# Two-block transformer kernel: the first three units on x without its norm, paired down units, residual updates on VectorE

## Chip, cores, metric

The kernel runs on one NeuronCore of one Trainium2 chip. The metric is the device time of one execution in microseconds.

## What is computed

Input `x` is 512 tokens by 1024 features in float32. Two pre-norm blocks follow each other, each with a feed-forward part with squared ReLU, and then a third block with three conditioned sublayers:

```python
# first block, two layers (mixer 0: dilated attention; mixer 1: latent attention)
h = rms_norm(x, norm_mix[i]); x = x + mixer(h)
h = rms_norm(x, norm_ffn[i]); x = x + sq_relu_mlp(h, w1[i], w2[i])
# second block: three sublayers (SwiGLU, attention + recurrence, SwiGLU)
h = rms_norm(x, g[2*j]) * (1 + scale) + shift
x = x + res_w * gate * rms_norm(fn(h), g[2*j + 1])
```

`rms_norm` divides each token by the root of its mean square and multiplies each feature by a gain. The mixers use 8 heads; each head of the first one has three query, three key and three value projections of 128 columns.

## The kernel before

Activations lie transposed, features on the 128 partitions, in 8 tiles `x[:, k, :]` of 512 tokens. Every weight matrix is streamed in units of 128 x 1024 (8 tiles of 128 x 128; `UNITS` of them in one order). A unit is used in split precision: ScalarE copies `raw` to `w_hi` in the rounded type fp32r (`split`, L893), the difference goes to `w_lo` (`low`: L1397 on VectorE in the attention of the first mixer, L369 on GpSimd from `U_AO + 2` on), and TensorE does three matmuls for each of the 8 steps k (L448, L449, L450: high by high, high by low, low by high). Activations are split in the same way (`h_hi`, `h_lo`). `unit` runs one unit, `unit_pair` two with their steps interleaved. Loads go out on SyncE's queue; `load_unit(u)` waits for `lo` of unit u - 3, `split(u)` for the matmuls of unit u - 3.

Each engine has one program, written out by hand, and each waits on counted semaphores (`after(name, index)`). The order within an engine is the order of the code. The parts that matter here:

- Start: `x` is squared tile by tile (`squares`, L900), summed over partitions by TensorE (L474), `inverse_root` (Ln and Exp, L921 and L923) gives the norm, `norm` makes `h_hi` and `h_lo` step by step, and then `pre_v` links (L1415 to L1431) compute a few columns of `small` from `lru_lambda` and the lambdas. The first head `a_head(0, 0, attend=False)` follows with nine units (3 queries, 3 keys, 3 values). Each query or key unit is evacuated to `a_raw` by ScalarE, squared, split, summed, normed and turned by `a_rope` (L1443 to L1456) on VectorE. Heads 1 to 7 then run as a loop in which each head projects while the one before attends. `a_head(1)` begins with unit 9.
- Feed-forward (`ffn`, two layers with four chunks each): 8 up units, `f_r` (Relu), `f_s` (square), `f_hi`, `f_lo` for each, then 8 down units that sum over the 8 tiles of `f_hi` and `f_lo`. Down unit 8 waits for `f_lo` tile by tile. VectorE also makes the conditioning (`ada_raw`, L1552) there; `condition` prepares its input.
- Sublayers: after SwiGLU or the mixer, `post_norm` scales `y` by its norm and adds it to `x`: tiles 0, 2, 3, 5, 6 on VectorE (L1799, L1801), tiles 1, 4, 7 on GpSimd (L397, L399). ScalarE squares each finished tile, TensorE sums, and `norm` makes the next input. The last `post_norm` is followed by the stores.

## Time and profile before

| | us |
|---|---|
| timed runs, median of 3 | 2627.26 (2626.61 to 2636.68) |
| profiled execution | 2632.38 |
| its span, first to last instruction | 2630.6 |
| TensorE (PE) busy | 2494.2 |
| VectorE (DVE) busy | 1270.8 |
| ScalarE (ACT) busy | 1026.6 |
| GpSimd (POOL) busy | 870.6 |

The profile is of one execution. Its lines give a start, a duration, the engine (PEld is TensorE's weight load), the line of the kernel, the operation with output and inputs, and in brackets how long the engine had been idle and what ended that. Durations of matmuls overlap by pipelining: what counts is the distance between starts. A float32 matmul (not fp32r) shows as two passes.

### The profile page before, as it was taken

The numbers are of one execution on the slowest core, as the hardware profiler recorded it, in microseconds if no ns is written. First come the engines' busy times: TensorE is split into PE (matmuls) and PEld (weight loads), VectorE is DVE, ScalarE is ACT, GpSimd is POOL, SyncE is SP. The second block draws the span as 40 slices with busy tenths as digits, with TensorE's granted clock in tenths as the row PEclk, the third lists the DMA queues.
The fourth block names the chain that finished last, engine by engine and source line by source line (L and its number), as shares of the span: only waits on it lengthen the run. The fifth ranks groups of instructions, "written<-read, shape, count | busy, mean of one in ns | idle before, by whom it ended". The sixth has DMA issues, their size and how long they took to land.

```text
span 2630.6 us, 31399 instructions
## 1 busy us (share of the span) xinstructions
PE 2494.2 (95%) x11168; PEld 1960.5 (75%) x11168; DVE 1270.8 (48%) x1737; ACT 1026.6 (39%) x1532; POOL 870.6 (33%) x369
## 2 busy tenths in 40 slices
PE   5999999999999998999999999999989968999997
PEld 3888888877888874568888878888857646688885
DVE  4766666656435555657355463201164795311114
ACT  4555555533223333544233233222344564322222
POOL 0000000024445532014455444444435334344443
PEclk8999999999999998999999999999999989999998
DMA  3222222224434521004344432223212201222221
GB/s 123 82 73 74 78 72 73 79 89 154 157 129 144 168 88 48 0 9 170 126 145 167 153 107 88 98 91 105 99 57 86 67 9 64 72 96 96 96 96 64
DMA packets 71237, 249.46 MB, mean 95 GB/s; under 512 B 9824, under 2 KB 10336, under 8 KB 70752
## 3 DMA queue, kind: packets, MB, share of 16 engines
q1 hardware_dynamic: 68912, 247.28, 28.1%
q8 instruction: 70, 1.15, 0.2%
q10 hardware_dynamic: 2224, 0.79, 0.1%
q14 instruction: 31, 0.25, 0.0%
HBM read 245.94 MB, written 2.10 MB: 94 GB/s over the span
## 4 chain that ended last, share of the span: by engine, by line
PE 86%; DVE 7%; issue 3%; ACT 2%; POOL 1%; DMA 0%; SPq 0%; ACTq 0%; DVEq 0%; POOLq 0%
PE psum L448 25%; PE psum L450 25%; PE psum L449 25%; PE psum L492 2%; PE psum L744 1%; DVE f_lo L1545 1%; PE psum L743 1%; PE psum L758 1%; PE psum L524 1%; PE psum L488 1%; PE psum L543 1%; PE psum L550 1%; DVE small L1912 1%; PE psum L817 1%; DVE y L1799 0%
## 5 line engine op out<-in xcount | busy, mean ns | idle before, releaser
L369 POOL TENSOR_TENSOR w_lo<-raw,w_hi 128x1024 fp32r<-128x1024 f32 x311 | 794.3, 2557 | 1559.1 <-ACT w_hi L893 1559.1
L448 PE MATMUL psum<-h_hi,w_hi 128*128 128x512 f32 x1856 | 740.0, 399 | 29.8 <-DVE a_k L1503 16.5
L450 PE MATMUL psum<-h_hi,w_lo 128*128 128x512 f32 x1856 | 726.4, 391 | 0.0
L449 PE MATMUL psum<-h_lo,w_hi 128*128 128x512 f32 x1856 | 725.9, 391 | 0.0
L893 ACT ACTIVATE w_hi<-raw 128x1024 fp32r<-128x1024 f32 x385 | 406.1, 1056 | 614.6 <-PE psum L450 614.3
L448 PEld LDWEIGHTS psum<-h_hi,w_hi 128*128 128x128 f32 x1856 | 351.2, 189 | 109.3 <-issue 35.4
L449 PEld LDWEIGHTS psum<-h_lo,w_hi 128*128 128x128 f32 x1856 | 351.3, 189 | 74.5 <-issue 3.4
L450 PEld LDWEIGHTS psum<-h_hi,w_lo 128*128 128x128 f32 x1856 | 350.6, 189 | 74.6
L1781 DVE TENSOR_TENSOR s_s<-s_g,psum 128x512 f32<-128x512 f32 x44 | 30.2, 687 | 399.9 <-PE psum L450 399.9
L448 PE MATMUL psum<-f_hi,w_hi 128*128 128x512 f32 x512 | 200.1, 391 | 9.4 <-DVE f_lo L1545 9.4
L450 PE MATMUL psum<-f_hi,w_lo 128*128 128x512 f32 x512 | 199.2, 389 | 0.0
L449 PE MATMUL psum<-f_lo,w_hi 128*128 128x512 f32 x512 | 199.2, 389 | 0.0
L448 PE MATMUL psum<-s_hi,w_hi 128*128 128x512 f32 x352 | 136.9, 389 | 0.0
L449 PE MATMUL psum<-s_lo,w_hi 128*128 128x512 f32 x352 | 136.9, 389 | 0.0
L450 PE MATMUL psum<-s_hi,w_lo 128*128 128x512 f32 x352 | 136.9, 389 | 0.0
L1569 DVE TENSOR_TENSOR nrm<-psum,rst 128x512 f32<-128x512 f32 x64 | 44.2, 690 | 171.7 <-PE psum L450 171.7
L1021 ACT ACTIVATE f_r<-psum 128x512 f32<-128x512 f32 x64 | 38.2, 597 | 223.4 <-PE psum L450 223.4
L962 ACT ACTIVATE a_raw<-psum 128x512 f32<-128x512 f32 x64 | 38.3, 598 | 211.9 <-PE psum L450 211.9
L448 PEld LDWEIGHTS psum<-f_hi,w_hi 128*128 128x128 f32 x512 | 96.1, 188 | 32.5 <-DVE f_lo L1545 12.8
L1552 DVE CUSTOM_DVE_ANT_0 ada_raw<-ada_raw,crow 128x1024 f32<-128x1024 f32 x72 | 117.4, 1630 | 0.0
L1542 DVE TENSOR_TENSOR f_s<-f_r,psum 128x512 f32<-128x512 f32 x64 | 43.7, 684 | 142.5 <-ACT f_r L1021 141.7
L450 PEld LDWEIGHTS psum<-f_hi,w_lo 128*128 128x128 f32 x512 | 96.1, 188 | 20.1
(286 smaller groups left out, 3399.5 us busy)
## 6 DMA issues: line engine op xcount, KB each, us to landing
raw<-stream SPq DMA_DIRECT2D x385, 512.0 KB, 3.3
ada_raw<-ada_in SPq DMA_DIRECT2D x72, 512.0 KB, 3.6
x<-x_in SPq DMA_DIRECT2D x2, 1024.0 KB, 6.4
out<-x SPq DMA_DIRECT2D x8, 256.0 KB, 2.0
a_mask<-mask_in SPq DMA_DIRECT2D x1, 1024.0 KB, 10.8
crow<-crow_in SPq DMA_DIRECT2D x2, 512.0 KB, 4.4
gatew<-gate_in ACTq DMA_DIRECT2D x2, 256.0 KB, 3.8
a_cos<-rope_in SPq DMA_DIRECT2D x1, 256.0 KB, 9.4
```

The costliest lines, as they stand in the source:

```text
L369: nc.gpsimd.tensor_tensor(w_lo[:, sl, :], raw[:, sl, :], f32(w_hi[:, sl, :]), ALU.subtract) \
L448: nc.tensor.matmul(o, whi, xh, start=start, stop=False)
L449: nc.tensor.matmul(o, whi, xl, start=False, stop=False)
L450: return nc.tensor.matmul(o, wlo, xh, start=False, stop=stop)
L492: last = nc.tensor.transpose(o[:, b * P:(b + 1) * P], src[:, b * P:(b + 1) * P], ident[:])
L893: A(w_hi[:, slot(u0), :], raw[:, slot(u0), :], ACT.Copy).then_inc(S["hi"], 1)
L962: A(a_raw[:, (par + j) % 2, :], bank((par + j) % 2), ACT.Copy).then_inc(S["A_evac"], 1)
L1021: A(f_r[:, j % 2, :], bank(j % 4), ACT.Relu).then_inc(S["F_r"], 1)
L1542: V.tensor_tensor(f_s[:, j % 2, :], f_r[:, j % 2, :], bank(j % 4), ALU.mult).then_inc(S["F_s"], 1)
L1552: V.tensor_tensor_reduce(out=ada_raw[:, j % 3, :], in0=ada_raw[:, j % 3, :], in1=crow[:], scale=1.0, scalar=0.0, op0=ALU.mult, op1=ALU.add ...
L1569: V.tensor_tensor(nrm[:, 1, :], down, rst[:, 1, :], ALU.mult).then_inc(S["F_t"], 1)
L1781: V.tensor_tensor(s_s[:, q % 2, :], s_g[:, q % 2, :], bank((2 * jj + 1) % 6), ALU.mult).then_inc(S["Sw_s"], 1)
```

## The change

Three things are changed.

1. The first three units (now one value and two query projections of head 0; `parts` is reordered so) run on `x` times its gain, split into `a_oh` and `a_ol`, without the division by the norm. That factor is one number per token, so VectorE multiplies the finished units by it (`first_scaled`). The sums of squares are collected on VectorE and summed by two matmuls between units 1 and 2. Head 0 is written out anew with its own order on all engines. Loads are reordered: `x`'s first half first. The chain on `lru_lambda` goes from the start to the place behind `condition(0)`.
2. In each feed-forward chunk down units 8 and 9 run as a `unit_pair`.
3. `post_norm` runs all 8 tiles on VectorE. The table load in front of its Ln moves into SwiGLU's second half, at unit 22.

```diff
 
         FFN_IN = ((h_hi, h_lo), (g_hi, g_lo))
 
-        POOL_TILES = (1, 4, 7)
-        VECTOR_TILES = (0, 2, 3, 5, 6)
-
         def y_added(yy, k, step=1):
 
-            tiles, name = (POOL_TILES, "Y_p") if k in POOL_TILES else (VECTOR_TILES, "Y_x")
-            return after(name, 2 * (len(tiles) * yy + tiles.index(k)) + step)
+            return after("Y_x", 2 * (KT * yy + k) + step)
...
@@ -313,13 +309,14 @@
+            sp.dma_start(x[:, 0:4, :], x_in[:, 0:4, :]).then_inc(S["x_in0"], 16)
+            sp.dma_start(cols[:], cols_in).then_inc(S["col_in"], 16)
+            load_unit(0, 0, 0)
+            sp.dma_start(x[:, 4:8, :], x_in[:, 4:8, :]).then_inc(S["x_in1"], 16)
+            load_unit(1, 1, 0)
+            sp.dma_start(ones[:], consts_in[0]).then_inc(S["par_in"], 16)
             sp.dma_start(small[0:64, 8:12], lam_in).then_inc(S["par_in"], 16)
-            sp.dma_start(cols[:], cols_in).then_inc(S["par_in"], 16)
-            sp.dma_start(ones[:], consts_in[0]).then_inc(S["par_in"], 16)
-            for q in range(2):
-                sp.dma_start(x[:, 4 * q:4 * q + 4, :], x_in[:, 4 * q:4 * q + 4, :]).then_inc(S[f"x_in{q}"], 16)
-            for u in range(3):
-                load_unit(u, slot(u), 0)
+            load_unit(2, 2, 0)
...
@@ -390,16 +387,7 @@
-            def post_norm(yy):
-
-                pool.wait_ge(*after("Y_rst", yy))
-                for k in POOL_TILES:
-                    nc.gpsimd.tensor_tensor(y[:, k, :], y[:, k, :], rst[:, 1, :], ALU.mult).then_inc(S["Y_p"], 1)
-                    pool.wait_ge(*y_added(yy, k, 0))
-                    nc.gpsimd.tensor_tensor(x[:, k, :], x[:, k, :], y[:, k, :], ALU.add).then_inc(S["Y_p"], 1)
-
             lows(R3, U_MI + 2, 3)
-            post_norm(0)
...
@@ -433,10 +421,7 @@
-            lows(U_MO + 2, U_S2 + 2, 3)
-            post_norm(1)
-            lows(U_S2 + 2, UNITS, 3)
-            post_norm(2)
+            lows(U_MO + 2, UNITS, 3)
@@ -556,12 +541,8 @@
...
-                        first = not attend
-                        if first and j == 0:
-                            unit_pair(U_A, (0, 1), (bank(0), bank(1)), h_hi, h_lo, norm_ready(0))
-                        elif not first or j >= 2:
-                            pe.wait_ge(*after("A_evac", n - 2))
-                            unit(U_A + n, j % 3, bank((par + j) % 2), h_hi, h_lo)
+                        pe.wait_ge(*after("A_evac", n - 2))
+                        unit(U_A + n, j % 3, bank((par + j) % 2), h_hi, h_lo)
                         if j >= 1:
                             a_post(h, j - 1, par)
@@ -606,9 +587,11 @@
                             collected_sums("N", 1 + 2 * layer)
                     elif 2 <= j < 8:
                         unit(u0 + 16 * i + j, sl, bank(j % 4), *FFN_IN[layer])
-                    elif j >= 8:
-                        unit(u0 + 16 * i + j, sl, bank(j % 4), f_hi, f_lo,
-                             (lambda k: after("F_lo", 8 * c + k)) if j == 8 else None)
+                    elif j == 9:
+                        unit_pair(u0 + 16 * i + 8, (slot(u0 + 8), sl), (bank(0), bank(1)), f_hi, f_lo,
+                                  lambda k: after("F_lo", 8 * c + k))
+                    elif j >= 10:
+                        unit(u0 + 16 * i + j, sl, bank(j % 4), f_hi, f_lo)
...
@@ -650,15 +633,48 @@
                 if half == 1:
                     collected_sums("Y", 2 * ph)
 
-            for k in range(KT):
-                if k == 0:
-                    pe.wait_ge(S["par_in"], 48)
-                square_sums(0, k)
+            def first_sum(j, free):
+
+                pe.wait_ge(*free)
+                pe.wait_ge(*after("A_sl", j))
+                c = slice((j % 2) * T, (j % 2 + 1) * T)
+                nc.tensor.matmul(bank(7), ones_r[:], w_hi[:, 3, c], start=True, stop=False)
+                nc.tensor.matmul(bank(7), ones_r[:], w_lo[:, 3, c], start=False, stop=True).then_inc(S["A_ms"], 1)
+
+            def first_value(p, src, free=None):
+
+                if free is not None:
+                    pe.wait_ge(*free)
+                pe.wait_ge(*after("A_evac", p))
+                transposes(src, bank(6), RES).then_inc(S["A_vt"], 1)
+
+            unit(0, 0, bank(0), a_oh, a_ol, lambda k: after("E_lo", k))
+            unit(1, 1, bank(1), a_oh, a_ol)
+            pe.wait_ge(S["par_in"], 32)
+            collected_sums("N", 0)
+            unit(2, 2, bank(2), a_oh, a_ol)
             pe.wait_ge(*after("pre_v", 0))
             nc.tensor.matmul(bank(5, 2), ones[0:64, :], small[0:64, 12:14], start=True, stop=True).then_inc(S["pre_p"], 1)
+            unit_pair(3, (0, 1), (bank(3), bank(4)), h_hi, h_lo, norm_ready(0))
+            first_sum(0, after("N_ln", 0))
+            pe.wait_ge(*after("pre_a", 0))
+            unit(5, 2, bank(5), h_hi, h_lo)
             pe.wait_ge(S["tab_in"], 16 * 4)
+            first_value(0, a_vc)
+            first_sum(1, after("A_ln", 0))
+            pe.wait_ge(*after("A_evac", 0))
+            unit(6, 0, bank(0), h_hi, h_lo)
+            first_sum(2, after("A_ln", 1))
+            pe.wait_ge(*after("A_evac", 1))
+            unit(7, 1, bank(1), h_hi, h_lo)
+            first_sum(3, after("A_ln", 2))
+            first_sum(4, after("A_ln", 3))
+            pe.wait_ge(*after("A_evac", 6))
+            unit(8, 2, bank(0), h_hi, h_lo)
+            first_sum(5, after("A_ln", 4))
+            first_value(7, a_raw[:, 1, :], after("A_V", 0))
             pe.wait_ge(*after("A_pad", 0))
-            a_head(0, 0, attend=False)
+            pe.wait_ge(*after("A_ln", 5))
             with pe.Fori(0, 3) as i:
                 a_head(2 * i + 1, 1)
                 a_head(2 * i + 2, 0)
...
@@ -1050,6 +1066,8 @@
...
                         A(s_hi[:, j // 2 - 1, :], s_s[:, q % 2, :], ACT.Copy).then_inc(S["Sw_hi"], 1)
+                    if half == 1 and j == 22:
+                        act.preload_act_table_set("natural_log_exp_and_others")
@@ -1062,7 +1080,6 @@
...
             def post_norm(yy, nn):
-                act.preload_act_table_set("natural_log_exp_and_others")
                 act.wait_ge(*after("Y_ms", 2 * yy + 1))
                 inverse_root(bank(7), rst[:, 1, :], D, "Y_ln", yy, "Y_rst")
@@ -1072,24 +1089,69 @@
...
-            act.wait_ge(S["par_in"], 48)
+            act.wait_ge(S["col_in"], 16)
+
+            def first_high(k):
...
+
+            def first_split(j):
+                act.wait_ge(*after("A_evac", j + 1))
+                act.wait_ge(*after("A_ms", j - 2))
+                A(sq[:, j % 2, :], a_raw[:, j % 2, :], ACT.Square).then_inc(S["A_sq"], 1)
+                act.wait_ge(*after("A_sq", j))
+                A(w_hi[:, 3, (j % 2) * T:(j % 2 + 1) * T], sq[:, j % 2, :], ACT.Copy).then_inc(S["A_sh"], 1)
+
+            def first_evac(j, p, b, free):
+                act.wait_ge(*after("mm", U_A + p))
+                act.wait_ge(*after("A_qn", free))
+                A(a_raw[:, j % 2, :], bank(b), ACT.Copy).then_inc(S["A_evac"], 1)
+
+            def first_root(j):
+                act.wait_ge(*after("A_ms", j))
+                act.wait_ge(*after("A_qn", j - 2))
+                inverse_root(bank(7), rst[:, j % 2, :], P, "A_ln", j, "A_rst")
+
+            for k in range(4):
+                first_high(k)
+            split(0)
+            for k in range(2):
+                first_square(k)
+            for k in range(4, KT):
+                first_high(k)
+            split(1)
+            for k in range(2, KT):
+                first_square(k)
+            split(2)
+            split(3)
+            act.wait_ge(*after("N_ms", sum_event(0)))
+            inverse_root(bank(7), a_s[:, 0, :], D, "N_ln", 0, "N_rst")
+            split(4)
+            act.wait_ge(S["par_in"], 32)
+            A(ones_r[:], ones[:], ACT.Copy)
             for k in range(KT):
-                squares(0, k, x[:, k, :], (S[f"x_in{k // 4}"], 16))
-            split(0)
-            split(1)
-            norm(0, None)
-            lam = COLS["lru_lambda"][0]
+                act.wait_ge(*scaled(0, k))
+                A(h_hi[:, k, :], nrm[:, k % 2, :], ACT.Copy).then_inc(S["N_hi"], 1)
+                if k == 3:
+                    first_split(0)
+            first_split(1)
             act.wait_ge(*after("pre_v", 0))
             act.wait_ge(*after("pre_p", 0))
             A(small[:, 14:16], bank(5, 2), ACT.Exp).then_inc(S["pre_a"], 1)
-            A(small[:, 16:24], cols[:, lam:lam + 8], ACT.Abs).then_inc(S["pre_a"], 1)
-            act.wait_ge(*after("pre_a", 1))
-            A(small[:, 24:32], small[:, 16:24], ACT.Exp, scale=-1.0).then_inc(S["pre_a"], 1)
-            act.wait_ge(*after("pre_v", 1))
-            A(small[:, 16:24], small[:, 32:40], ACT.Ln).then_inc(S["pre_a"], 1)
-
-            A(ones_r[:], ones[:], ACT.Copy)
-            a_head(0, 0, attend=False)
+            split(5)
+            first_root(0)
+            for j in range(2, 6):
+                first_evac(j, j + 1, (0, 0, 3, 4, 5, 0)[j], j - 2)
+                first_split(j)
+                split(j + 4)
+                first_root(j - 1)
+            split(10)
+            first_root(5)
+            first_evac(7, 7, 1, 5)
+            first_evac(8, 8, 0, 5)
...
@@ -1097,6 +1159,13 @@
             a_head(8, 0, project=False)
             outward(U_AO, ("R_x", 0), 1)
             condition(0)
+            lam = COLS["lru_lambda"][0]
+            A(small[:, 16:24], cols[:, lam:lam + 8], ACT.Abs).then_inc(S["pre_a"], 1)
+            act.wait_ge(*after("pre_a", 1))
+            A(small[:, 24:32], small[:, 16:24], ACT.Exp, scale=-1.0).then_inc(S["pre_a"], 1)
+            act.wait_ge(*after("pre_v", 1))
+            A(small[:, 16:24], small[:, 32:40], ACT.Ln).then_inc(S["pre_a"], 1)
+
...
@@ -1404,33 +1473,58 @@
                 ins.then_inc(S["pre_v"], 1)
...
-            dve.wait_ge(S["par_in"], 48)
+            def first_low(k):
+                dve.wait_ge(*after("E_hi", k))
+                V.scalar_tensor_tensor(out=a_ol[:, k, :], in0=x[:, k, :], scalar=col("norm_mix", k), in1=f32(a_oh[:, k, :]),
+                                       op0=ALU.mult, op1=ALU.subtract).then_inc(S["E_lo"], 1)
+            def first_scaled(p, out, src, r):
+                dve.wait_ge(*after("mm", U_A + p))
+                return V.tensor_tensor(out, src, r, ALU.mult)
...
+            dve.wait_ge(S["col_in"], 16)
+            for k in range(4):
+                first_low(k)
+            low(0, 0)
+            collect("N", 0, 1)
+            for k in range(4, KT):
+                first_low(k)
+            low(1, 1)
+            for k in range(2, 7):
+                collect("N", 0, k)
+            low(2, 2)
+            low(3, 0)
+            V.memset(a_k0[:, :, 0:64], 0.0)
+            V.memset(a_k0[:, :, 64 + T:], 0.0).then_inc(S["A_pad"], 1)
+            dve.wait_ge(S["par_in"], 32)
             link(V.tensor_tensor(small[0:64, 12:14], small[0:64, 8:12:2], small[0:64, 9:12:2], ALU.mult))
-            low(0, 0)
-            low(1, 1)
-            norm(0, lambda k: col("norm_mix", k))
...
-            dve.wait_ge(*after("pre_a", 2))
-            link(V.tensor_scalar(u_, e_, 1.0, None, ALU.add))
...
-            assert pre[0] == PRE_V
-
+            dve.wait_ge(*after("N_rst", 0))
+            v0 = bank(0).rearrange("p (r i) -> p r i", r=RES)
+            rv = r0.rearrange("p (r i) -> p r i", r=RES)
+            first_scaled(0, a_vc[:, 64:T].rearrange("p (i r) -> p r i", r=RES), v0[:, :, 0:112], rv[:, :, 0:112])
+            first_scaled(0, a_vc[:, 0:64].rearrange("p (i r) -> p r i", r=RES), v0[:, :, 112:128], rv[:, :, 112:128]).then_inc(S["A_evac"], 1)
+            first_scaled(1, a_raw[:, 0, :], bank(1), r0).then_inc(S["A_evac"], 1)
+            low(4, 1)
+            for k in range(4):
+                first_norm(k)
+            first_scaled(2, a_raw[:, 1, :], bank(2), r0).then_inc(S["A_evac"], 1)
+            for k in range(4, KT):
+                first_norm(k)
+            first_norm_low(7)
@@ -1499,10 +1593,23 @@
...
 
-            V.memset(a_k0[:, :, 0:64], 0.0)
-            V.memset(a_k0[:, :, 64 + T:], 0.0).then_inc(S["A_pad"], 1)
+            def first_token_values(i, j):
+                dve.wait_ge(*after("A_vt", i))
+                V.tensor_copy(a_v[:, j, :], bank(6)).then_inc(S["A_V"], 1)
+
+            a_square_low(0, 0)
+            a_square_low(0, 1)
+            low(5, 2)
             dve.wait_ge(S["tab_in"], 16 * 4)
-            a_head(0, 0, attend=False)
+            a_rope(0, 0, 0)
+            first_token_values(0, 0)
+            for j in range(2, 6):
+                a_square_low(0, j)
+                low(j + 4, (j + 4) % 3)
+                a_rope(0, j - 1, 0)
+            low(10, 1)
+            a_rope(0, 5, 0)
+            first_token_values(1, 1)
@@ -1574,6 +1681,28 @@
 
             outward(U_AO, 1)
             condition(0)
+            e_, u_, w_, z_ = small[:, 24:32], small[:, 32:40], small[:, 40:48], small[:, 48:56]
+            lam = cols[:, COLS["lru_lambda"][0]:COLS["lru_lambda"][0] + 8]
+            dve.wait_ge(*after("pre_a", 2))
+            link(V.tensor_scalar(u_, e_, 1.0, None, ALU.add))
...
+            link(V.tensor_tensor(small[:, 57:58], small[:, 15:16], small[:, 14:15], ALU.subtract))
+            link(V.tensor_scalar(small[:, 56:57], small[:, 57:58], -LAMBDA_INIT, None, ALU.add))
+            link(V.tensor_scalar(small[:, 58:59], col("subln"), 1.0 - LAMBDA_INIT, None, ALU.mult))
+            assert pre[0] == PRE_V
@@ -1795,7 +1924,7 @@
             def post_norm(yy):
 
                 dve.wait_ge(*after("Y_rst", yy))
-                for k in VECTOR_TILES:
+                for k in range(KT):
                     V.tensor_tensor(y[:, k, :], y[:, k, :], rst[:, 1, :], ALU.mult).then_inc(S["Y_x"], 1)
                     dve.wait_ge(*y_added(yy, k, 0))
```

## Rows read from the trace of the kernel before

**Rows 1.** The page, busy time by engine, with share of the span and instructions.

```profile
PE 2494.2 (95%) x11168; PEld 1960.5 (75%) x11168; DVE 1270.8 (48%) x1737; ACT 1026.6 (39%) x1532; POOL 870.6 (33%) x369
```

**Rows 2.** Windows: length, busy time of each engine, PEclk, DMA share, GB/s.

```profile
0.00:35.50 35.50, 10.33 (x19) 3.82 (x19) 16.09 (x36) 16.06 (x27) 0.19 (x4) 0.84 0.50 186
...
35.00:41.00 6.00, 5.53 (x13) 4.40 (x14) 0.31 (x2) 0.00 (x0) 0.00 (x0) 0.50 0.00 0
```

**Rows 3.** TensorE's waits: total us, times, longest.

```profile
PE psum L448 <- DVE f_lo L1545: 9.4, 8, 1.2
```

**Rows 4.** Timeline of the start: start, duration, engine, line, operation.

```profile
0.72 0.57 SPq L316 DMA_DIRECT2D small<-lam_in  x1
...
2.43 0.91 SPq L320 DMA_DIRECT2D x<-x_in  x2
...
7.88 1.15 ACT L900 ACTIVATE sq<-x 128x512 f32<-128x512 f32 x2 [5.79 <-DMA x<-x_in]
...
35.47 0.77 PE L448 MATMUL psum<-h_hi,w_hi 128*128 128x512 f32 x1 [16.52 <-DVE a_k L1503]
...
94.86 0.48 PE L448 MATMUL psum<-h_hi,w_hi 128*128 128x512 f32 x1
```

**Rows 5.** Timeline around the first residual update.

```profile
1940.08 1.12 PE L482 MATMUL psum<-sq,ones 128*128 128x512 f32 x2 [0.58 <-ACT sq L911]
1940.79 1.28 ACT L1065 ACT_TABLE_LOAD   x1
...
1943.47 0.69 DVE L1799 TENSOR_TENSOR y<-y,rst 128x512 f32<-128x512 f32 x1 [1.96 <-ACT rst L923]
...
1944.19 1.64 DVE L1801 TENSOR_TENSOR x<-x,y 128x512 f32<-128x512 f32 x1
...
1954.22 0.69 DVE L1801 TENSOR_TENSOR x<-x,y 128x512 f32<-128x512 f32 x1
...
1955.55 0.69 DVE L1801 TENSOR_TENSOR x<-x,y 128x512 f32<-128x512 f32 x1
...
1956.96 1.98 PE L474 MATMUL psum<-sq,ones 128*128 128x512 f32 x4 [0.20 <-ACT sq L900]
```

**Rows 6.** Timeline of VectorE in the start: norm steps, a subtraction, one rope.

```profile
20.80 1.41 DVE L1374 SCALAR_TENSOR_TENSOR nrm<-x,cols,rst 128x512 f32<-128x512 f32 x2
...
22.24 0.69 DVE L1365 TENSOR_TENSOR h_lo<-nrm,h_hi 128x512 fp32r<-128x512 f32 x1
...
30.57 1.47 DVE L1365 TENSOR_TENSOR h_lo<-nrm,h_hi 128x512 fp32r<-128x512 f32 x2
...
51.22 1.22 DVE L1397 TENSOR_TENSOR w_lo<-raw,w_hi 128x1024 fp32r<-128x1024 f32 x1
...
55.04 0.75 DVE L1443 SCALAR_TENSOR_TENSOR nrm<-a_raw,cols,rst 128x512 f32<-128x512 f32 x1
...
57.98 0.69 DVE L1456 TENSOR_TENSOR a_qk<-nrm,a_t 128x512 f32<-128x512 f32 x1
```

**Rows 7.** Timeline at the first down unit of a chunk.

```profile
642.10 3.16 POOL L369 TENSOR_TENSOR w_lo<-raw,w_hi 128x1024 fp32r<-128x1024 f32 x1 [2.28 <-ACT w_hi L893]
...
645.19 0.39 PE L448 MATMUL psum<-f_hi,w_hi 128*128 128x512 f32 x1
...
645.87 0.39 PE L448 MATMUL psum<-f_hi,w_hi 128*128 128x512 f32 x1
...
651.29 0.50 PE L448 MATMUL psum<-f_hi,w_hi 128*128 128x512 f32 x1 [1.18 <-DVE f_lo L1545]
```

**Rows 8.** Timeline at the entry of the first feed-forward stage.

```profile
602.93 1.04 ACT L893 ACTIVATE w_hi<-raw 128x1024 fp32r<-128x1024 f32 x1
...
610.38 1.23 DVE L1531 TENSOR_TENSOR crow<-crow,cexp 128x1024 f32<-128x1024 f32 x1
...
612.10 0.79 PE L448 MATMUL psum<-h_hi,w_hi 128*128 128x512 f32 x1
```

**Rows 9.** Timeline of the last addition.

```profile
2626.82 0.69 DVE L1801 TENSOR_TENSOR x<-x,y 128x512 f32<-128x512 f32 x1
```

60 lines of the change are left out of this document (36 added, 24 removed).

## Prediction

> **What bounds the kernel now.** I read the page first. TensorE is busy for 95% of a span of 2630.6 us [rows 1], so a change can only pay where TensorE stands or runs at half clock. Two views then say where that is. The windows by stage show the first 35.5 us with 10.3 us of TensorE work, and after them 6 us at a granted clock of 0.50, the lower of its two levels (1.2 GHz) [rows 2]. The list of TensorE's waits shows eight waits for `f_lo` of 9.4 us in total [rows 3]. The timeline shows the rest. In the start, `x` is issued at 2.43 us and squared from 7.88 on; the norm is built step by step, and the first matmul of a weight unit starts at 35.47 us after 16.5 us of idling; the first unit of head 1 starts at 94.86 us [rows 4]. From there on the seven heads are a steady loop, so 94.86 is the mark against which I measure the start. In the residual stage at 1940 us TensorE has nothing but short sums until 1958.9 [rows 5].
>
> **The prices.** On VectorE a 128x1024 subtraction takes 1.22 us, one step of the norm (scale, low part) repeats every 1.39 us ((30.57 - 22.24) / 6), the first low part is ready 2.13 us after the norm starts (22.24 + 0.69 - 20.80), and one rope takes 3.6 us (57.98 + 0.69 - 55.04) [rows 6]. A unit is 8 steps of 0.68 us (645.87 - 645.19) [rows 7], so 5.44 us at full clock and 10.9 at half. A split on ScalarE takes 1.04 us [rows 8].
>
> **Change 1, the start.** I follow the four queues as the new code orders them.
> 1. `x`'s first half took 5.4 us from issue to use (7.88 - 2.43) and is now issued first, at 0.72 [rows 4]: it is there at about 6.1 us.
> 2. ScalarE makes four high parts, 0.6 us apart, then split(0), 1.04; VectorE subtracts, 1.22: 6.1 + 2.4 + 1.1 + 1.3 = 10.9 us. Unit 0 starts there, 24.6 us before the old first unit. That is not the gain, since the norm has to be made anyway.
> 3. TensorE was at the lower level from 35.47 to about 41.0 [rows 2, 4]. I charge the same 5.5 us here: unit 0 takes 8.2 us, to 19.1. Unit 1 ends at 24.5, the two sums of squares (0.43 x 4) at 26.2, unit 2 at 31.7.
> 4. Logarithm and exponential, 1.3 us, give the norm at 27.6. Now VectorE has three scalings of finished units and low(4): 0.6 + 0.2 + 0.7 + 1.2, to 30.4, and then 2.13 us to the first low part: 32.6. TensorE waits 0.8 us. The pair (units 3, 4) is paced by VectorE at 1.39 us a step against 1.36 of work, with one scaling of 0.7 put in: it ends at 44.3.
> 5. From here VectorE is the narrow place, because its queue does in order what TensorE needs out of order. A sum and unit 5 (its low part is late by 0.5 us) end at 50.6; transposes and a sum, 51.8. VectorE, after the first rope, stands waiting for these transposes to copy the value tile, and only then makes the low part of unit 6: 54.0, a stall of 2.3 us. Unit 6 ends at 59.4, unit 7 at 65.3. Unit 8 goes to bank 0 and needs it evacuated, which needs the first operation of the fourth rope: 68.9, stalls of 1.0 and 1.7 us. It ends at 74.3. The last value tile needs a slot that the first operation of the sixth rope frees, and two ropes of 3.6 us and low(10) lie ahead of it: 78.9, a stall of 4.2 us. Transposes, and head 1 starts at 79.5.
>
> The start gives 94.86 - 79.5 = 15.4 us. Bounds: if `x` lands at 8 as before, all of it slips by 2 to 3 us (gain 12.5); if the five stalls of step 5 (together 9.7 us) did not occur at all, the gain would be 25. I keep 12 to 19 for the range, since each stall follows from the order in the code.
>
> **The part of it that is moved.** The `lru_lambda` chain leaves the start and goes behind `condition(0)`. On ScalarE its last logarithm waits for VectorE's first link, and VectorE comes to that only after a reciprocal and a product, which end at 611.6 us. ScalarE did a split at 602.93 [rows 8]; this one, of the third unit of the feed-forward stage, is now queued behind the logarithm: 612.1 + 1.07, then 2.4 on GpSimd, 615.7 us. TensorE started that unit at about 612.5. So **+3.2 us**; the splits behind it come 2.5 us or more ahead of their units. Bounds: 0, if ScalarE's wait is met early by something I overlook, and 5, if the 15 links on VectorE (3 us) make another unit late. The 15 links themselves lie beside units 2 and 3.
>
> **Change 2, the pair of down units.** Unit 8 stands 1.18 us before its last step in each of eight chunks [rows 7], 9.4 us in all [rows 3]. As a pair, the last step begins 14 x 0.68 = 9.5 us after the start instead of 4.8, so the wait for `f_lo` is gone. But the pair now waits at its start for the low part of unit 9, which unit 8 alone did not need: GpSimd makes it from 642.10, 3.16 us long, to 645.26, and unit 7's last step ends at 645.19 [rows 7]. That is 0.1 us per chunk, with no slack. Unit 8 ends later than before, so split(11) comes at the pair's end: 1.1 + 2.5 to 3.2 us, inside unit 10's 5.44. **-9.4 + 0.8 = -8.6 us**. Bounds: -9.4 with no wait; -4 if the low part comes 0.6 us later in each chunk.
>
> **Change 3, the residual updates.** While GpSimd works too, an operation on VectorE takes 1.64 us; before and after, 0.69 [rows 5]. So they take turns, and dividing the work gives nothing. Alone, VectorE does one tile (two operations) every 1.33 us (1955.55 - 1954.22). From 1943.47 on the eighth tile is then ready after 7 x 1.33 + 1.41 = 10.7 us, against 12.8 now; squares and sums behind it end 1.85 us later (0.7 of square, 1.1 of two passes), at 12.6 us, where they now end at 15.5 (1956.96 + 1.98 - 1943.47). **-2.9 us** in each of the two norms that follow. GpSimd loses its part; nothing queued there waited for it, since its next piece comes after the whole norm, whose sums end at 1958.9 [rows 5].
> The table load moves from behind the last square to the down units of SwiGLU, where ScalarE idles. The last sum ends at 1940.08 + 1.12 = 1941.20 and the logarithm could start then; the load holds it to 1942.07 [rows 5]: **-0.9 us** in three places. The Trainium skill (ScalarE: Activation LUTs, What ACT_TABLE_LOAD costs) puts a switch of tables at 1.28 us plus a drain of 1.38. This trace agrees with the first figure and shows no drain: the load starts where the operation before it ends. By the page the three places would give about 4 us more and the time would be 4 us lower than I forecast.
> At the end of the kernel: 12.8 - 10.7 = 2.1, the load 0.9, and one store to issue after the last tile instead of two, 0.4. The tail behind the last addition is 3.1 us now [rows 9]. **-3.4 us**. The bounds for all of change 3 (-11.0) are -7, if TensorE's sums run at the lower level (1.7 us a tile against 1.33) and the next pair too, and -12.
>
> **Sum.** -15.4 + 3.2 - 8.6 - 2 x 3.8 - 3.4 = -31.8 us. Against the profiled execution, 2632.4 us with its span of 2630.6, that is 2600.6. The three timed runs are 2626.6, 2627.3 and 2636.7, so the profiled one lies 5 us above their median. I forecast 2627.3 - 31.8 = 2595.5 us.
>
> **The rivals.**
> - The start loses more than I count (A): the stalls behind VectorE's order come on top of a later landing of `x`, and during the 4 us stall before head 1 the clock falls, which would make the next 3 to 6 us run at half rate as it did behind 35.47. 10 us less gain: 2605. For it: six matters in a row hang on VectorE. Against: each was priced.
> - The moved chain and the pair cost nothing, and VectorE keeps up at the start (B): 3.2 + 0.8 + some 5 of the stalls: 2586. For it: VectorE is free for most of the first 30 us. Against: the order in the queues.
> - The pair's new wait (C) takes the place of the old one. GpSimd's product has no slack at 645.2. If the pair stood w us in each chunk, the FFN part would be 8w - 9.4. It eats the whole change at w = (31.8 + 0.8) / 8 = 4.1 us, a split that came after unit 7 instead of unit 6 (5.4 us late). Then the time is 2627.3 - 31.8 + 8 x 5.4 - 0.8 = 2638, no change by the bound below. Against: ScalarE issues that split before it waits for unit 7.
> - The slow operations are VectorE's own (D), slower than before. If 1.64 us were the price of these operations and not that of sharing, 16 of them would take 26.2 us against 12.8: +13.4 instead of -2.1 to -2.9, three times, 48 us above my forecast: 2643. Without change 3's 7.9 us on VectorE 23.9 are left, and they are used up at (12.8 + 23.9 / 3) / 16 = 1.3 us per operation. Against: the operations after GpSimd's last are 0.69 [rows 5].
> - It does not do what it says (E): the wait for `f_lo` stays because the low part of unit 7 comes later still. Price 9.4: 2605, inside the range.
>
> **Chances.** My forecast 0.70, A and E 0.13, B 0.10, C 0.04, D 0.03. A measurement of this kernel tells a change from none beyond about 0.5%, 13 us. The first three cases are all faster than that: 0.93; C is 0.04; slower 0.03. The range takes in A and B: 2585 to 2607.
>
> **What the new profile shows if I am right.** The first weight matmul near 11 us, with TensorE at half rate for about 5 us; the first unit of head 1 near 79.5, with a wait of about 4 us before it on the copy of the value tile. A wait of about 3 us at the third unit of the first feed-forward stage, for GpSimd. No wait for `f_lo`, and at most 0.1 us for `w_lo` at each pair. All 16 residual operations on VectorE at 0.69 us, and sums that end 12.6 us after the first. **What would make it wrong:** a head 1 that starts after 84 us, a wait of 1 us at the pairs, or residual operations over 1 us.

## The result, and the profile after

The changed kernel takes 2603.94 us (median of 4 runs, 2603.11 to 2607.41); the kernel before took 2629.53 beside it (4 runs, 2626.61 to 2636.68). The ratio is 0.9895, 95% interval 0.9878 to 0.9913: faster by 1.05%. The forecast was 2595.5 us and faster; the time lies 8.4 us above it and inside the range. A second measurement of the same kernel (below) gave 2601.62 us and 0.9890 (0.9871 to 0.9910).

The profiled execution took 2607.41 us with a span of 2605.6. Its page, busy time by engine:

```profile
PE 2493.5 (96%) x11156; PEld 1961.2 (75%) x11156; DVE 1292.1 (50%) x1773; ACT 1028.4 (39%) x1535; POOL 845.1 (32%) x351
```

TensorE has as much to do as before [rows 1]; 25.0 us of standing are gone (2630.6 - 2605.6). Timeline of the start, which answers to [rows 4]:

```profile
6.34 2.56 ACT L1096 ACTIVATE a_oh<-x,cols 128x512 fp32r<-128x512 f32 x4 [4.25 <-DMA cols<-cols_in]
...
11.16 0.79 PE L433 MATMUL psum<-a_oh,w_hi 128*128 128x512 f32 x1 [11.16 <-DVE w_lo L1466]
...
33.27 0.47 PE L433 MATMUL psum<-h_hi,w_hi 128*128 128x512 f32 x1 [0.63 <-DVE h_lo L1497]
...
54.38 0.51 PE L433 MATMUL psum<-h_hi,w_hi 128*128 128x512 f32 x1 [2.14 <-DVE w_lo L1466]
...
70.97 0.50 PE L433 MATMUL psum<-h_hi,w_hi 128*128 128x512 f32 x1 [1.41 <-ACT a_raw L1111]
...
81.77 0.91 PE L477 MATMUL psum<-ident,a_raw 128*128 128x128 f32 x4 [3.01 <-ACT a_raw L1111]
...
82.33 0.78 PE L433 MATMUL psum<-h_hi,w_hi 128*128 128x512 f32 x1
```

Unit 0 starts at 11.16 us (10.9 was forecast), the pair at 33.27 (32.6), and the stalls stand where step 5 of the forecast put them: 2.1 us before unit 6, 1.4 before unit 8, 3.0 before the last value tile. Head 1 starts at 82.33, not at 79.5. Timeline of the entry of the first feed-forward stage [rows 8]:

```profile
599.93 0.21 ACT L1167 ACTIVATE small<-small 128x8 f32<-128x8 f32 x1 [8.47 <-DVE small L1687]
...
600.05 1.04 ACT L909 ACTIVATE w_hi<-raw 128x1024 fp32r<-128x1024 f32 x1
...
601.17 4.68 POOL L366 TENSOR_TENSOR w_lo<-raw,w_hi 128x1024 fp32r<-128x1024 f32 x2 [14.80 <-ACT w_hi L909]
601.19 2.35 DVE L1695 TENSOR_TENSOR small<-small 128x8 f32<-128x8 f32 x1
...
603.66 0.47 PE L433 MATMUL psum<-h_hi,w_hi 128*128 128x512 f32 x1 [2.90 <-POOL w_lo L366]
```

ScalarE's logarithm (L1167) stood 8.47 us for VectorE's links with the split behind it; the split starts at 600.05, GpSimd's low part at 601.17, and TensorE stands 2.90 us. That is the sequence of the forecast. Timeline of the first residual update [rows 5]:

```profile
1925.36 1.12 PE L467 MATMUL psum<-sq,ones 128*128 128x512 f32 x2 [0.58 <-ACT sq L927]
1926.52 0.69 ACT L937 ACTIVATE rst<-psum,cols 128x512 f32<-128x512 f32 x1 [0.46 <-PE psum L467]
...
1927.90 0.69 DVE L1928 TENSOR_TENSOR y<-y,rst 128x512 f32<-128x512 f32 x1 [1.12 <-ACT rst L939]
1928.63 0.69 DVE L1930 TENSOR_TENSOR x<-x,y 128x512 f32<-128x512 f32 x1
...
1940.51 0.69 ACT L937 ACTIVATE rst<-psum,cols 128x512 f32<-128x512 f32 x1 [1.22 <-PE psum L459]
```

Each operation takes 0.69 us, the logarithm no longer stands behind a table load, and the next one comes 12.6 us after the first operation (1940.51 - 1927.90), as forecast.

TensorE's units come in the same order in both kernels, so the lead of matching units (how much earlier a unit starts than in the kernel before) says where the time came from:

| stage | forecast | profiled executions |
|---|---|---|
| start, until the heads run steadily | -15.4 | -11.1 |
| end of the last head (549 us) | 0 | -0.8 |
| entry of the feed-forward part | +3.2 | +4.7 |
| feed-forward layers 0 and 1 | -8.6 | -4.5 and -4.5 |
| entry of the mixer between them (960 us) | 0 | +1.5 |
| residual updates 1, 2 and the last | -3.8, -3.8, -3.4 | -3.1, -3.6, -3.5 |
| sum | -31.8 | -25.0 |

The 0.8 us at 549 us are not the change's: in this trace of the kernel before some steps there run at the lower clock (PEclk 0.57 from 549 to 553 us), and in the run "start back" the same code has 1.00 there.

### The profile page after: what moved, and what is told of

Its sections match the earlier page's. It is cut to its first block, busy times and chain, and to the rows that moved or that the text cites. A ratio compares the mean times of both kernels' runs of the same rounds, so it can differ in the third digit from the quotient of the medians.

```text
span 2605.6 us, 31398 instructions
## 1 busy us (share of the span) xinstructions
PE 2493.5 (96%) x11156; PEld 1961.2 (75%) x11156; DVE 1292.1 (50%) x1773; ACT 1028.4 (39%) x1535; POOL 845.1 (32%) x351
## 4 chain that ended last, share of the span: by engine, by line
PE 87%; DVE 5%; issue 5%; ACT 2%; POOL 1%; DMA 0%; ACTq 0%; POOLq 0%; DVEq 0%; SPq 0%
PE psum L433 26%; PE psum L435 25%; PE psum L434 25%; PE psum L477 1%; PE psum L760 1%; POOL w_lo L366 1%; PE psum L759 1%; PE psum L774 1%; PE psum L509 1%; PE psum L473 1%; DVE small L2041 1%; PE psum L535 0%; PE psum L528 0%; PE psum L833 0%; DVE m_w L2036 0%
## 5 line engine op out<-in xcount | busy, mean ns | idle before, releaser
L433 PE MATMUL psum<-h_hi,w_hi 128*128 128x512 f32 x1832 | 732.3, 400 | 20.0 <-DVE h_lo L1436 11.9
L435 PE MATMUL psum<-h_hi,w_lo 128*128 128x512 f32 x1832 | 719.1, 393 | 0.0
L434 PE MATMUL psum<-h_lo,w_hi 128*128 128x512 f32 x1832 | 718.7, 392 | 0.0
L434 PEld LDWEIGHTS psum<-f_lo,w_hi 128*128 128x128 f32 x512 | 96.1, 188 | 19.7
```

Source lines behind the costliest of these rows:

```text
L433: nc.tensor.matmul(o, whi, xh, start=start, stop=False)
L434: nc.tensor.matmul(o, whi, xl, start=False, stop=False)
L435: return nc.tensor.matmul(o, wlo, xh, start=False, stop=stop)
```

## The experiments

Twelve kernels ran, the changed one twice. "Head 1" is the start of its first unit; the last column is the length of TensorE's stage from 970 to 1159 us, whose code is the same in all, against that of the changed kernel's first profile.

| kernel | median us | ratio to before (95%) | head 1 | 970 to 1159 |
|---|---|---|---|---|
| changed | 2603.94 | 0.9895 (0.9878 to 0.9913) | 82.33 | 0 |
| changed, again | 2601.62 | 0.9890 (0.9871 to 0.9910) | 82.26 | -4.1 |
| without the pair | 2612.46 | 0.9925 (0.9908 to 0.9941) | 82.38 | +0.1 |
| GpSimd back | 2612.67 | 0.9929 (0.9914 to 0.9944) | 82.22 | -5.8 |
| table load back | 2604.67 | 0.9899 (0.9882 to 0.9916) | 79.31 | 0 |
| start back | 2611.33 | 0.9930 (0.9912 to 0.9947) | 92.85 | -2.7 |
| before, chain moved | 2631.88 | 1.0005 (0.9996 to 1.0015) | 90.29 | 0 |
| logarithm later | 2599.70 | 0.9877 (0.9856 to 0.9898) | 79.42 | +0.1 |
| stalls filled | 2599.02 | 0.9879 (0.9860 to 0.9899) | 79.64 | -2.8 |
| copy later | 2601.58 | 0.9887 (0.9871 to 0.9904) | 79.59 | -2.6 |
| and bank 2 | 2600.59 | 0.9881 (0.9863 to 0.9899) | 79.19 | -5.8 |
| and own buffer | 2596.32 | 0.9861 (0.9843 to 0.9879) | 73.62 | +0.1 |
| and logarithm later | 2593.41 | 0.9856 (0.9837 to 0.9875) | 73.79 | -2.7 |

**The same kernel again.**

> The changed kernel once more, unaltered, as the neighbour of the three others of this call. The traces so far show the same start code with head 1 starting at 82.3 us in one execution and near 79.4 in two others, and single runs of both kernels lie some 4 to 5 us apart. If half-clock stretches that fall differently from execution to execution are the reason, this trace differs from the first one only in steps of TensorE at granted clock 0.50; if something else of the change varies (a transfer, VectorE's order), the waits themselves have other lengths.

The waits have the same lengths: 2.15, 0.78, 1.40 and 3.01 us in the start, 2.90 at the entry. All of the difference of the spans (2605.6 against 2601.4) lies in the stage from 970 to 1159 us. Windows of the changed kernel, first execution and then second (length, busy PE, PEld, DVE, ACT, POOL, PEclk, DMA share, GB/s):

```profile
1008.00:1012.00 4.00, 0.78 (x4) 0.35 (x3) 3.97 (x4) 1.41 (x2) 2.35 (x1) 0.80 0.00 0
1012.00:1016.00 4.00, 4.00 (x8) 2.48 (x8) 2.35 (x4) 0.00 (x0) 0.00 (x0) 0.50 0.43 131
1016.00:1020.00 4.00, 3.52 (x11) 2.19 (x11) 1.95 (x4) 1.20 (x2) 0.00 (x0) 0.85 0.00 0
```

```profile
1008.00:1012.00 4.00, 0.79 (x4) 0.30 (x3) 3.96 (x4) 1.19 (x2) 2.34 (x1) 1.00 0.00 0
1012.00:1016.00 4.00, 3.50 (x15) 2.40 (x14) 3.37 (x7) 1.20 (x2) 0.00 (x0) 1.00 0.43 131
1016.00:1020.00 4.00, 3.03 (x11) 1.84 (x11) 3.19 (x5) 1.61 (x3) 0.31 (x1) 1.00 0.02 4
```

The same work runs at the lower level in one execution and at the upper in the other. TensorE is busy for 0.8 of 4 us just before, in both. Over all kernels this stage took one of four lengths, about 0, 2.7, 4.1 or 5.8 us shorter, and head 1 of the unaltered start came at 79.3 to 79.4 or at 82.2 to 82.4. A single trace of this kernel is therefore uncertain by up to 6 us, and I judge small edits by the stage that they touch.

**Without the pair.**

```diff
-                    elif j == 9:
-                        unit_pair(u0 + 16 * i + 8, (slot(u0 + 8), sl), (bank(0), bank(1)), f_hi, f_lo,
-                                  lambda k: after("F_lo", 8 * c + k))
-                    elif j >= 10:
-                        unit(u0 + 16 * i + j, sl, bank(j % 4), f_hi, f_lo)
+                    elif j >= 8:
+                        unit(u0 + 16 * i + j, sl, bank(j % 4), f_hi, f_lo,
+                             (lambda k: after("F_lo", 8 * c + k)) if j == 8 else None)
```

> The changed kernel with down units 8 and 9 of each feed-forward chunk one after the other again. My theory (the wait for f_lo was 9.4 us over eight chunks and the pair costs about 0.6 us at its starts): the span becomes 8.9 us longer, and eight waits of about 1.2 us for f_lo come back before the last step of unit 8. Rival (the wait had only moved within the chunk and would be met by something else now that the start is different): less than 3 us.

The list of TensorE's waits has the old row back [rows 3]:

```profile
PE psum L433 <- DVE f_lo L1650: 9.4, 8, 1.2
```

The two layers are longer by 4.5 us each, 9.1 in all, and the median is 8.5 us above the changed kernel's first one and 10.8 above its second. The pair is worth what was forecast. Its own wait for the second low part is small: in the changed kernel a pair's first matmul starts 0.35 or 0.55 us after the last one of unit 7, where 0.23 is a step without a wait, so the pair stands 0.1 us in four chunks and 0.3 in the other four. The two profiled spans lie only 6.7 us apart (2612.3 - 2605.6), since this trace lacks 1.5 us that the changed kernel loses at 960 us (below).

**GpSimd and the table load back in the residual updates.**

```diff
+        POOL_TILES = (1, 4, 7)
+        VECTOR_TILES = (0, 2, 3, 5, 6)
...
+            def post_norm(yy):
+
+                pool.wait_ge(*after("Y_rst", yy))
+                for k in POOL_TILES:
...
-                for k in range(KT):
+                for k in VECTOR_TILES:
```

> The changed kernel with residual tiles 1, 4 and 7 on GpSimd again; the moved table load stays moved. My theory (the two engines take turns, an operation on VectorE takes 1.64 us beside GpSimd and 0.69 alone): 2.9 us longer in each of the first two residual stages and 2.5 at the end, 8.3 us in all. Rival (the gain of the stages came from the table load, and dividing the work costs nothing): the operations take 0.69 us beside GpSimd too, and the time changes by less than 2 us.

Timeline of its first residual update:

```profile
1923.19 0.69 DVE L1946 TENSOR_TENSOR y<-y,rst 128x512 f32<-128x512 f32 x1 [1.12 <-ACT rst L957]
1923.92 1.63 DVE L1948 TENSOR_TENSOR x<-x,y 128x512 f32<-128x512 f32 x1
...
1938.71 0.69 ACT L955 ACTIVATE rst<-psum,cols 128x512 f32<-128x512 f32 x1 [1.50 <-PE psum L477]
```

15.5 us to the logarithm (1938.71 - 1923.19) against 12.6: the 2.9 us of the forecast. In the second update it is 16.2 against 12.6, and at the end 3.5 us, of which 2.0 are the operations and 1.5 the stores behind them. With the load away the operations still take 1.63 us, so the rival falls. Sharing the work with GpSimd costs 10 us in the three places (2.9 + 3.6 + 3.5), where 8.3 were expected. The excess is not explained: with the same division the kernel before needed 15.5 us in the second update and 3.1 us behind its last addition, where this run needs 16.2 and 4.0.

```diff
-                    if half == 1 and j == 22:
-                        act.preload_act_table_set("natural_log_exp_and_others")
...
             def post_norm(yy, nn):
+                act.preload_act_table_set("natural_log_exp_and_others")
```

> The changed kernel with the table load in front of post_norm's logarithm again. My theory: 0.9 us in each of three places, 2.7 us. Rival 1 (a drain of about 1.4 us comes with each load, as the Trainium skill says in ScalarE: Activation LUTs, What ACT_TABLE_LOAD costs): about 2.3 us in each place, 6.9 us. Rival 2 (the load fits beside TensorE's last sums): 0.

```profile
1922.27 1.13 PE L467 MATMUL psum<-sq,ones 128*128 128x512 f32 x2 [0.58 <-ACT sq L927]
1922.98 1.28 ACT L1081 ACT_TABLE_LOAD   x1
...
1925.65 0.69 DVE L1927 TENSOR_TENSOR y<-y,rst 128x512 f32<-128x512 f32 x1 [1.96 <-ACT rst L939]
```

From the last sum to VectorE's first operation 3.38 us pass instead of 2.54: 0.8, where 0.9 was forecast, and no drain. But the unit pair behind the norm ran fewer of its steps at the lower clock, and of the three times 0.8 to 1.0 us a net 0.3, 0.4 and 0.8 were left in the lead of the units. The median, 2604.67 against 2603.94 and 2601.62, doesn't tell it from nothing.

**The start back, and the chain alone.** The first takes the diffs of the pair and of `post_norm` alone, on the kernel before. The second is this, with VectorE's 15 links moved in the same way:

```diff
-            A(small[:, 16:24], cols[:, lam:lam + 8], ACT.Abs).then_inc(S["pre_a"], 1)
-            act.wait_ge(*after("pre_a", 1))
-            A(small[:, 24:32], small[:, 16:24], ACT.Exp, scale=-1.0).then_inc(S["pre_a"], 1)
-            act.wait_ge(*after("pre_v", 1))
-            A(small[:, 16:24], small[:, 32:40], ACT.Ln).then_inc(S["pre_a"], 1)
...
             condition(0)
+            A(small[:, 16:24], cols[:, lam:lam + 8], ACT.Abs).then_inc(S["pre_a"], 1)
+            act.wait_ge(*after("pre_a", 1))
+            A(small[:, 24:32], small[:, 16:24], ACT.Exp, scale=-1.0).then_inc(S["pre_a"], 1)
+            act.wait_ge(*after("pre_v", 1))
+            A(small[:, 16:24], small[:, 32:40], ACT.Ln).then_inc(S["pre_a"], 1)
```

> The kernel before with changes 2 and 3 only: start and lru_lambda chain as before. My theory (start -12 to -15 us, chain +3 to +4): 8 to 12 us slower than the changed kernel, 14 to 17 faster than before. Rival (the early start only moves work, and what it gains is lost by the end): within 3 us of the changed kernel.

It is 9.7 us slower than the changed kernel beside it (2611.33 - 2601.62). Its head 1 starts at 92.85, 2.0 us earlier than the same code did in the profile of before [rows 4]. Of these, 0.7 are there at the first matmul of a weight unit (34.76 against 35.47), and 1.0 is lost from 50 to 54 us, where that profile had the granted clock at 0.66 and this one has 1.00.

> The kernel before with one edit: the lru_lambda chain moved behind condition(0). My prediction had +3.2 us at the entry of the feed-forward part (third unit late by a split that is queued behind the chain's logarithm). In the start the chain lies beside TensorE's first pair, so at most 3 us of VectorE's and ScalarE's work leave the start; I expect head 1 to start 0 to 3 us earlier. Net 0 to +4 us. Rival (the chain costs nothing at its new place): 0 to -3 us.

Head 1 comes 2.6 us earlier than with the chain in place (92.85 - 90.29), but not for the reason expected. The chain did not lie beside TensorE's first pair, it stood ahead of it: the pair waits for a memset of `a_k0` that VectorE comes to only after the 15 links [rows 4], and without them it starts at 32.19 instead of 34.76. A memset ahead of the links should give the same without the cost at the entry; no run tried it. TensorE stands at the entry as in the changed kernel:

```profile
32.19 0.76 PE L448 MATMUL psum<-h_hi,w_hi 128*128 128x512 f32 x1 [13.48 <-DVE a_k L1481]
...
610.20 0.50 PE L448 MATMUL psum<-h_hi,w_hi 128*128 128x512 f32 x1 [2.89 <-POOL w_lo L369]
```

Its entry is 4.7 us longer, the amount of the changed kernel. In sum the move costs 2.1 us by the traces (4.7 - 2.6); the time does not change measurably.

**The logarithm later.** ScalarE's last logarithm of the chain goes behind the first split and Relu of the first chunk.

```diff
+                    if first and layer == 0 and j == 0:
+                        act.wait_ge(*after("pre_v", 1))
+                        A(small[:, 16:24], small[:, 32:40], ACT.Ln).then_inc(S["pre_a"], 1)
...
-            act.wait_ge(*after("pre_v", 1))
-            A(small[:, 16:24], small[:, 32:40], ACT.Ln).then_inc(S["pre_a"], 1)
```

> The changed kernel with the last logarithm of the lru_lambda chain issued later on ScalarE, behind the first split and the first Relu of the first feed-forward chunk, so that the split no longer stands behind it. My theory (the split of the third unit was late by the wait of that logarithm for VectorE's links, and TensorE stood 2.9 us for the low part and then ran at half clock for a while): 3 to 4 us shorter, and the wait for the low part near 604 us is gone. Rival (the third unit is late for the links on VectorE or for its load, not for the split): no change.

The split now starts at 590.02 us, 8.8 us before the unit that needs it; the wait and the half-clock steps behind it are gone, and TensorE gains 4.3 us at the entry. The median is 4.2 and 1.9 us below the two of the changed kernel. The remaining 0.4 us are lost at the fifth unit of the chunk, which waits for its low part; VectorE's links may be what delays that, which was not tried.

**The stalls filled.**

```diff
+            def fill(n, b):
+                for _ in range(n):
+                    nc.tensor.matmul(bank(b), h_hi[:, 0, 0:128], h_hi[:, 0, :], start=True, stop=True)
...
-            pe.wait_ge(*after("A_evac", 0))
+            pe.wait_ge(*after("A_evac", 2))
+            fill(8, 2)
             unit(6, 0, bank(0), h_hi, h_lo)
...
+            fill(5, 2)
             pe.wait_ge(*after("A_evac", 6))
             unit(8, 2, bank(0), h_hi, h_lo)
             first_sum(5, after("A_ln", 4))
+            fill(12, 2)
```

At the entry ten such matmuls go in front of the third unit.

> The changed kernel with extra matmuls, whose results are not used, in the stalls of TensorE: 8 before unit 6 (stall of 2.1 us), 5 before unit 8 (1.4), 12 before the last value tile (3.0), 10 before the third unit of the first feed-forward chunk (2.9). At 0.23 us each they fit into the stalls, so no stall ends earlier. Theory (the steps at granted clock 0.50 behind these stalls follow from TensorE's idling): the clock stays at 1.00 behind them, head 1 starts at 79 to 80 us, and the feed-forward entry gains another 1 us; 3 to 5 us faster than the changed kernel where that one has all the stretches, 1 to 2 us where it has few. Rival (the clock falls there for another reason): the stretches stay, and the extra matmuls cost 0 to 3 us.

Windows of the changed kernel's second execution, then of this one:

```profile
54.00:58.00 4.00, 3.77 (x10) 2.99 (x11) 3.87 (x7) 2.81 (x4) 0.00 (x0) 0.57 0.44 131
...
70.00:74.00 4.00, 3.22 (x9) 2.54 (x10) 3.87 (x7) 3.77 (x6) 0.00 (x0) 0.68 0.42 133
...
82.00:86.00 4.00, 4.00 (x14) 3.25 (x13) 2.20 (x4) 0.90 (x1) 0.00 (x0) 0.61 0.14 56
```

```profile
54.00:58.00 4.00, 4.00 (x19) 3.29 (x19) 3.87 (x7) 2.81 (x4) 0.00 (x0) 1.00 0.37 131
...
70.00:74.00 4.00, 4.00 (x19) 3.33 (x18) 3.93 (x6) 3.10 (x4) 0.00 (x0) 1.00 0.02 6
...
82.00:86.00 4.00, 4.00 (x24) 3.10 (x26) 0.00 (x0) 0.49 (x1) 0.00 (x0) 1.00 0.00 0
```

The three half-clock stretches are gone, and head 1 starts at 79.64 us. The steps right behind it run at full clock too, so that by the second unit of head 1 this kernel leads the changed one's second execution by 3.9 us. The entry gains 1.6 us, with its stall as long as before:

```profile
596.12 2.88 PE L591 MATMUL psum<-h_hi 128*128 128x512 f32 x10
599.54 0.50 PE L433 MATMUL psum<-h_hi,w_hi 128*128 128x512 f32 x1 [0.54 <-POOL w_lo L366]
```

The median is 2.6 us below the changed kernel's beside it. How much does one trace show, where the clock varies by itself? At the entry all nine traces that have the stall lose 4.7 us, and this one 3.1. Behind the last stall of head 0 the clock was down in all six traces of the unaltered start, and not here. Behind the stall before unit 6 it stayed up in two of those six, so at that place the filled trace alone proves nothing. So at the entry and before head 1 it is TensorE's idling that brings the lower clock, as the Trainium skill has it in general (TensorE: Matmul & The Clock Gate, HAM oscillation), here with stalls of 2.9 and 3.0 us; matmuls for nothing bring part of it back.

**The order of head 0.** Three edits, each on top of the one before.

```diff
-            first_token_values(0, 0)
             for j in range(2, 6):
                 a_square_low(0, j)
                 low(j + 4, (j + 4) % 3)
+                if j == 2:
+                    first_token_values(0, 0)
...
-            pe.wait_ge(*after("A_evac", 6))
-            unit(8, 2, bank(0), h_hi, h_lo)
+            pe.wait_ge(*after("A_evac", 2))
+            unit(8, 2, bank(2), h_hi, h_lo)
...
-            first_value(7, a_raw[:, 1, :], after("A_V", 0))
+            first_value(7, a_s[:, 1, :], after("A_V", 0))
...
+            act.wait_ge(*after("mm", U_A + 7))
+            A(a_s[:, 1, :], bank(1), ACT.Copy).then_inc(S["A_evac"], 1)
```

> The changed kernel, but in head 0 VectorE copies the first value tile behind the low part of unit 6 instead of ahead of it. My theory (VectorE stood waiting for transposes that come after unit 5, and made unit 6's low part only then; the stall of 2.2 us before unit 6 comes from this order): unit 6 starts 2 us earlier. The steps at half clock behind the stall (about 55 to 58 us) may go with it, another 1 to 1.5 us. Since the later stalls come from VectorE's ropes, part of it is lost again there: head 1 starts 1 to 3 us earlier. Rival (VectorE's total work in head 0 sets the start of head 1, and order within it doesn't matter): unit 6 starts earlier and head 1 does not.

```profile
52.79 0.47 PE L433 MATMUL psum<-h_hi,w_hi 128*128 128x512 f32 x1 [0.70 <-DVE w_lo L1466]
...
78.85 1.08 PE L477 MATMUL psum<-ident,a_raw 128*128 128x128 f32 x4 [3.01 <-ACT a_raw L1111]
```

The stall before unit 6 fell from 2.1 to 0.7 us. Head 1 starts at 79.59, but the unaltered order reached 79.31 and 79.42 in the two executions whose clock stayed up behind unit 6's stall, so the gain at head 1 is not shown.

> As the run before, and unit 8 goes to PSUM bank 2 instead of bank 0, so that it waits for an evacuation that is long past and not for that of unit 6. My theory (the wait of 1.4 us before unit 8 is for bank 0): it goes, 1.4 us at that place. It comes back in the stall before head 1 (3.0 us, it grows), unless the half-clock stretch near 71.7 to 75.2 us goes too: head 1 starts 0 to 1.7 us earlier than in the run before. Rival (unit 8 is late by its own low part): no change even at unit 8.

```profile
78.45 1.09 PE L477 MATMUL psum<-ident,a_raw 128*128 128x128 f32 x4 [5.83 <-ACT a_raw L1111]
```

The stall before unit 8 is gone, the last one is 2.8 us longer, and head 1 starts at 79.19. What is won ahead of it is lost in this stall, which ends with the slot that VectorE's sixth rope frees; the next run takes that slot away.

> As the run before, and unit 7 (the last value unit) is evacuated at once to a buffer that is idle here, from which the transposes are made, instead of waiting for a slot that the sixth rope frees. My theory (the stall of 3.0 us before head 1, and the half-clock stretch behind it, come from this slot): the stall falls below 1 us and the granted clock stays up; head 1 starts 3 to 5 us earlier than in the run before. Rival (the rope of the sixth projection is needed by head 1 anyway): the stall only moves to the wait for the sixth sum, and nothing is gained.

```profile
73.62 0.49 PE L433 MATMUL psum<-h_hi,w_hi 128*128 128x512 f32 x1 [0.96 <-ACT rst L937]
...
80.85 0.65 PE L477 MATMUL psum<-ident,a_raw 128*128 128x128 f32 x4 [1.51 <-DVE a_v L1599]
```

With its own buffer, head 1 starts 5.6 us earlier; 1.7 come back when unit 9's transposes wait for VectorE's copy of the value tile before. By the time the heads run steadily this kernel leads the changed one (its first execution) by 8.4 us.

> As the run before, with the last logarithm of the lru_lambda chain issued later too. If the parts add up, 3 to 4 us shorter than the run before and 9 to 13 us shorter than the changed kernel: near 2592 us. Rival (a start that gains does not reach the end, since a later stage absorbs it): under 5 us shorter than the changed kernel.

In the traces the parts add up: 8.4 us from the start and 4.3 from the entry. By the medians the last step brought 2.9 us (2596.32 - 2593.41). It is the fastest kernel here, 10.5 and 8.2 us below the two medians of the changed one. The four runs of this section were made on another chip than the changed kernel's second measurement; the kernel before took 2633.12 us there (9 runs) and 2631.01 us on that other one, so the chips hardly differ.

## Why the prediction was right, and where it was off

**Right in mechanism.** The stalls of step 5 occurred, near the sizes forecast (2.1, 0.8, 1.4 and 3.0 us against 2.3, 1.0, 1.7 and 4.2). The stall at the entry was 2.90 us and put the third unit off by 3.5 us (5.00 us from the last matmul of the unit before it instead of 1.54), against 3.2. The wait for `f_lo` went (9.1 us when undone, 8.6 forecast), the sums of the residual update end 12.6 us after its first operation, and a table load costs 0.8 against 0.9. Rivals B to E did not occur: the moved chain does cost time and the stalls behind VectorE's order stand (B), the pair stands 0.1 to 0.3 us (C), the operations are 0.69 us (D), no wait for `f_lo` is left (E). The time lies within 1 us of rival A's 2605 and 8.4 us above the forecast, and A's lower clock behind the stalls is part of the reason. But A put its 10 us on the start alone, where 4.2 were lost; that its number fits is luck.

**Off in the start, by 4.2 us (-15.4 against -11.1).** The terms of steps 3 to 5 leave the clock up once it has risen. In the profiled execution it fell behind three stalls (PEclk 0.58 from 54 to 58 us, 0.72 from 70 to 74, 0.58 from 82 to 86). Head 1 started 2.8 us later than forecast (82.33), and 1.4 us more of the lead were gone by its second unit. In the runs "table load back" and "logarithm later" the same start code has 1.00 from 54 to 58 us, and head 1 starts at 79.31 and 79.42. Two things make that difference of 3 us. Unit 6 takes 7.6 us in the one case and 6.0 in the other: 1.6 us. And unit 0, at the lower level at the very start, took 8.4 us against 6.9 and 7.5 (8.2 were charged), so that the pair already starts 1.4 and 1.0 us later. The stretch behind the stall before unit 8 costs nothing at head 1, since the last stall takes it up: "logarithm later" has 1.00 from 70 to 74 us, and there that stall has just the 4.2 us of the forecast.

```profile
78.68 1.09 PE L477 MATMUL psum<-ident,a_raw 128*128 128x128 f32 x4 [4.20 <-ACT a_raw L1114]
```

The clock behind the last stall is rival A's second half. Its first half, a later landing of `x`, did not occur (used from 6.34 us on, 6.1 forecast). The old start was measured high too: 94.86 in the profile that the forecast used, 92.85 in another execution of the same code, so 2 of the 15.4 us were a loss of that one execution, which I took for the kernel's. Between the best trace of either start head 1 comes 13.5 us earlier (92.85 - 79.31). Some 2.6 of these are the chain that no longer stands ahead of the first pair; the forecast has them in its sum without naming them.

**Off at the entry, by 1.5 us.** The term of +3.2 has the stall alone. Behind it TensorE ran at half clock (PEclk 0.57 from 604 to 608 us), and filling the stall gave back 1.6 us of the 4.7. In the sum the start of the third unit stands as about 612.5, where the row has 612.10 [rows 8]; with that the term would have been 3.6, nearer to the 3.5 measured.

**Off at 960 us, by 1.5 us.** Nothing was forecast there. TensorE stands 2.83 us before a sum of that mixer in both kernels, and behind it the changed kernel runs at the lower clock (0.50 from 960 to 962 us), the kernel before doesn't:

```profile
959.61 2.07 PE L693 MATMUL psum<-sq,ones 128*128 128x512 f32 x2 [2.83 <-ACT sq L1194]
```

```profile
956.43 1.12 PE L693 MATMUL psum<-sq,ones 128*128 128x512 f32 x2 [2.83 <-ACT sq L1194]
```

The second row is of the run "copy later", whose code is the same there and which lost nothing: so it varies without a change. Over the fourteen traces the loss was 0 in four, 1.4 to 1.6 us in eight and 2.9 in two. But the three traces without the pair are all among the four, and of the eleven with it ten lost something. Whether the pair makes the fall more likely stays open.

**The rest, and the base.** Start, entry and 960 us make 7.2 us. The feed-forward layers gained 0.4 more than forecast and the residual updates 0.8 less; of these 0.7 lie at the first update, where the pair of units behind the norm ran at PEclk 0.52 from 1942 to 1949 us, against 0.76 in "table load back". The 0.8 us at 549 us count for the change without being its own. Together (7.2 - 0.4 + 0.8 - 0.8) these are the 6.8 us between -31.8 and -25.0. The other 1.6 of the 8.4 us are the two profiled executions, which lay 5.1 us above the median before and 3.5 after. The three runs on which the forecast stood had a median of 2627.26 us; 15 runs later on had 2631.01, in groups near 2627, 2632 and 2636.5. Against that base the change brought 29.4 us (2631.01 - 2601.62). That the groups come from the stage at 970 us, as in the changed kernel, is likely and was not shown, since only one trace of the kernel before exists.
